# Input projections of a two-layer decoder as three float32r products, with low parts made by adding DMAs

## The chip, the core and the metric

The kernel runs on one core of a Trainium2 chip. The metric is the time of one execution on the device, in microseconds (us), and a version stands for the median of its runs.

## The reference

One sequence of 512 tokens with 1024 channels passes two layers. Layer 0 normalises x, projects it with one matrix of 1024 x 2560 and splits the columns into five blocks of 512: the input u of a state-space mixer, and query, forget, input (here: value) and gate of a gated linear recurrence. Layer 1 is sliding-window attention. Behind each mixer stands a mixture of 16 experts. What the change touches is the beginning:

```python
h = rms_norm(x, even_mix_norm[j])
proj = jnp.einsum('bld,de->ble', h, even_in_proj[j])
u = proj[..., :S5_WIDTH]
hq, hf, hi, hg = jnp.split(proj[..., S5_WIDTH:], 4, axis=-1)
a_out = s5_mixer(u, ...)            # step = exp(log_step); mag = exp(lam_re * step); scan over the sequence
b_out = hgrn2_mixer(hq, hf, hi, hg, ...)   # f = lb + (1 - lb) * sigmoid(hf); cumsum(log f) in chunks of 32
mix = jnp.einsum('blc,cd->bld', jnp.concatenate([a_out, b_out], axis=-1), even_out_proj[j])
```

All of it is float32, and the result must keep nearly that precision.

## The kernel before

Everything is written out by hand: each engine has one program, and the order of its instructions is the order in the text. Semaphores join them. SyncE issues the loads of a stream of weight slots (128 partitions x 2048 float32, 1 MB each) into a ring of six; a slot is loaded again when a counter (slot_free, w_lo_done) says that its last reader is done.

**Preparation.** x is loaded in four tiles of 128 tokens, normalised by ScalarE and VectorE, turned by TensorE and scaled by VectorE into hT (8 blocks of 128 channels x 512 tokens; `scaled`, line 1012). Meanwhile GpSimd works out the state-space coefficients on tiles of 128x16: step by `exact_exp` (line 439, a polynomial with some 25 small instructions), the turn (line 480), mag by the same function (line 481), mag to the fourth power (line 484), then turn_hi and turn_lo, and, once the constants are in, one product of 128x2048 (line 503, RAW).

**Products.** A block is 8 matmuls over the channel blocks, 128x512 out. Both operands are float32, which TensorE does in two passes, so that a product counts as two instructions. Four blocks make u (line 1763), and proj(i) makes blocks 0 to 3 of forget, 4 to 7 of query, 8 to 11 of value and 12 to 15 of gate (lines 1785 to 1805). ScalarE copies each result out of PSUM (lines 727 and 734).

**The order on TensorE** after u is: proj(0), turn_inputs (1770), proj(1), inputs(0) (1807), proj(2), proj(3), make_taps (1820), proj(4), inputs(1), proj(5), readout(0) (1832), proj(6), proj(7), readout(1), proj(8), readout(2), proj(9), readout(3), proj(10), proj(11). Then come the heads of the recurrence: head_scores(0) (1874), the first half of proj(12), head_increments(0) (1890), and so on, with the gate blocks between them, up to the gated linear unit (line 1929).

**VectorE** makes the coefficients (from line 1057; it waits there for mag), turned inputs and phases, then for four groups products_in, the scans and their products (scan_and_products, line 1189). scan 2 needs readout(0) done, scan 3 needs readout(1) done. `skip(b)` (line 1207) adds the readout to u. Behind skip(2) stands `forget` (1213), then, after ScalarE's Ln (line 779), the running sums (`summed_logs`, 1221). GpSimd's `differences(h)` (line 507) follow the sums, ScalarE's `exponentials(h)` (749) the differences, VectorE's `keyed(h)` (1245) the exponentials; head_scores(h) reads what they made. ScalarE's keys_out(0) stands behind exponentials(3), and head_increments(0) needs it.

**The three-product form** is in use elsewhere in the kernel (the output projection, line 1984, and the experts): an operand a is split into a_hi, its copy in float32r (a shorter mantissa, one pass on TensorE), made by ScalarE, and a_lo = a - a_hi, made by VectorE; hi x hi, hi x lo and lo x hi are summed in PSUM.

## Time and profile before

| | us |
|---|---|
| median of 3 runs | 839.35 (838.61 to 840.06) |
| the profiled execution | 841.01 |
| its span | 839.3 |
| TensorE, VectorE, ScalarE, GpSimd busy in the span | 788.5, 599.5, 467.2, 164.2 |
| mean granted clock of TensorE | 0.986 of 2.4 GHz |

The span is the time that the hardware profiler saw from the first to the last instruction, and the execution's own time is measured around it. Times in the rows below are microseconds from the start of the span. Busy time of TensorE is given twice, for matmuls (PE) and for the loads of their stationary operand (PEld). Instructions of one kind in a row are merged into one line with their count. Matmuls overlap at their ends, so a count of them is best divided out of the chain of waits, which has no overlap.

### The profile page before, as it was taken

How to read it: one execution, taken by the hardware profiler on the slowest of the kernel's cores; microseconds unless marked ns; L12 is line 12 of the kernel's file. 1: busy time of each engine (PE TensorE's matmuls, PEld its weight loads, DVE VectorE, ACT ScalarE, POOL GpSimd, SP SyncE). 2: the span in 40 equal slices, each digit the busy share in tenths (PEclk: the TensorE clock that was granted, in tenths of full speed). 3: DMA queues.
4: the chain of work that ended last, by engine and by line, in shares of the span. 5: the costliest groups of instructions: out<-in, count | busy, mean ns of one | idle time of the engine just before them, and what ended most of it. 6: DMA issues, size and time to landing. Idle time of an engine off the chain costs nothing.

```text
span 839.3 us, 11098 instructions
## 1 busy us (share of the span) xinstructions
PE 788.5 (94%) x4236; PEld 553.4 (66%) x4236; DVE 599.5 (71%) x817; ACT 467.2 (56%) x637; POOL 164.2 (20%) x169
## 2 busy tenths in 40 slices
PE   5999999999999899989999899999999899999993
PEld 3455555555588878867777455556579778777872
DVE  4699974866553779877987566667645688887891
ACT  5033202823432478776885219677735387787791
POOL 4400001500001223422211000133101223323221
PEclk9999999999999799999999999999999999999998
DMA  9421120203462499999995400052063599989962
GB/s 363 158 94 58 45 100 2 101 1 123 189 221 118 160 390 367 317 329 319 316 335 174 201 0 1 4 197 102 1 275 136 188 418 338 311 318 337 320 204 39
DMA packets 31450, 160.93 MB, mean 192 GB/s; under 512 B 7601, under 2 KB 7729, under 8 KB 16032
## 3 DMA queue, kind: packets, MB, share of 16 engines
q1 hardware_dynamic: 18432, 130.03, 40.6%
q0 software_dynamic: 11232, 24.60, 10.4%
q10 hardware_dynamic: 1728, 5.52, 1.8%
q8 instruction: 38, 0.62, 0.3%
q14 instruction: 20, 0.16, 0.1%
HBM read 152.32 MB, written 24.12 MB: 210 GB/s over the span
## 4 chain that ended last, share of the span: by engine, by line
PE 55%; DMA 18%; DVE 14%; ACT 8%; issue 1%; POOL 1%; DVEq 1%; ACTq 0%; POOLq 0%; SPq 0%
DMA ring<-stream 17%; PE PS L1797 11%; PE PS L1984 8%; DVE w_lo L994 8%; PE PS L2233 7%; PE PS L2114 5%; PE PS L1763 3%; ACT w_hi L688 3%; PE PS L2139 3%; PE PS L2014 2%; PE PS L2268 2%; PE PS L1929 2%; PE PS L2291 1%; PE PS L1747 1%; PE PS L2281 1%
## 5 line engine op out<-in xcount | busy, mean ns | idle before, releaser
L994 DVE TENSOR_TENSOR w_lo<-ring,w_hi 128x2048 fp32r<-128x2048 f32 x92 | 209.9, 2289 | 42.7 <-ACT w_hi L688 37.7
L688 ACT ACTIVATE w_hi<-ring 128x2048 fp32r<-128x2048 f32 x86 | 164.7, 1917 | 50.6 <-DMA ring<-stream 48.1
L2114 PE MATMUL PS<-w_hi,left_hi 128*128 128x512 f32 x512 | 174.6, 403 | 7.9 <-DVE w_lo L994 5.8
L2114 PEld LDWEIGHTS PS<-w_hi,left_hi 128*128 128x128 f32 x512 | 96.1, 188 | 31.5 <-DVE w_lo L994 5.8
L2114 PE MATMUL PS<-w_lo,left_hi 128*128 128x512 f32 x256 | 100.1, 391 | 0.0
L2139 PE MATMUL PS<-w_hi,left_lo 128*128 128x512 f32 x256 | 85.4, 394 | 9.1 <-DVE left_lo L994 7.9
L2233 PE MATMUL PS<-ring,hT 128*128 128x512 f32 (+1 forms) x192 | 73.5, 527 | 0.3 <-DVE hT L994 0.3
L536 POOL DMA_INDIRECT arena<-rows x32 | 47.6, 1488 | 121.6 <-PE PS L2091 106.1
L2139 PEld LDWEIGHTS PS<-w_hi,left_lo 128*128 128x128 f32 x256 | 48.0, 188 | 22.2 <-DVE left_lo L994 10.8
L1797 PE MATMUL PS<-ring,hT 128*128 128x512 f32 x128 | 57.6, 599 | 0.4 <-ACT arena L734 0.4
L1797 PE MATMUL PS<-hT,ring 128*128 128x512 f32 x128 | 56.3, 595 | 0.0
L2114 PEld LDWEIGHTS PS<-w_lo,left_hi 128*128 128x128 f32 x256 | 48.3, 189 | 8.3
L2233 PEld LDWEIGHTS PS<-ring,hT 128*128 128x128 f32 x192 | 34.7, 190 | 28.8 <-issue 26.9
L1984 PE MATMUL PS<-w_lo,left_hi 128*128 128x512 f32 x128 | 50.6, 396 | 0.3 <-DVE left_lo L994 0.3
L2139 PE MATMUL PS<-w_lo,left_lo 128*128 128x512 f32 x128 | 49.9, 390 | 0.0
L734 ACT ACTIVATE arena<-PS 128x512 f32<-128x512 f32 x16 | 9.6, 599 | 71.5 <-PE PS L1797 71.5
L1984 PE MATMUL PS<-w_hi,left_hi 128*128 128x512 f32 x112 | 44.8, 400 | 0.0
L994 DVE TENSOR_TENSOR left_hi<-PS,left_hi 128x1024 fp32r<-128x1024 f32 (+1 forms) x35 | 40.3, 1156 | 5.4 <-ACT left_hi L841 2.3
L1984 PE MATMUL PS<-w_hi,left_lo 128*128 128x512 f32 x112 | 43.8, 391 | 0.0
L1797 PEld LDWEIGHTS PS<-hT,ring 128*128 128x128 f32 x128 | 23.9, 190 | 28.9 <-issue 28.6
L1797 PEld LDWEIGHTS PS<-ring,hT 128*128 128x128 f32 x128 | 23.4, 190 | 27.3 <-issue 26.2
L540 POOL DMA_INDIRECT out<-hT,rows x16 | 26.0, 1627 | 68.7 <-ACT hT L857 68.7
(274 smaller groups left out, 1363.2 us busy)
## 6 DMA issues: line engine op xcount, KB each, us to landing
ring<-stream SPq DMA_DIRECT2D x110, 1024.0 KB, 16.3
arena<-stream SPq DMA_DIRECT2D x6, 1024.0 KB
rows<-arena POOLq DMA_DIRECT2D x8, 512.0 KB, 3.0
x<-stream SPq DMA_DIRECT2D x4, 1024.0 KB
x<-x_in SPq DMA_DIRECT2D x4, 512.0 KB, 5.8
x<-x_in ACTq DMA_DIRECT2D x4, 512.0 KB, 4.2
sums<-x POOLq DMA_DIRECT2D x4, 512.0 KB, 3.9
x<-sums SPq DMA_DIRECT2D x4, 512.0 KB, 5.4
```

Source lines behind the costliest of these rows:

```text
L536: return pool.indirect_dma_start(xrow[j], None, rows_d[:, :], bass.IndirectOffsetOnAxis(index, 0), bounds_check=SEQ - 1, oob_is_err=False)
L540: return pool.indirect_dma_start((sums_d, out_d)[layer][:, :], bass.IndirectOffsetOnAxis(index, 0), rows, None, bounds_check=SEQ - 1, oob_ ...
L688: act.activation(w_hi[pair], held_slot(layer, m), ACT.Copy).then_inc(w_hi_done, 1)
L994: return V.tensor_tensor(out, a, b, op)
L1763: ins = mm(PS[:, 2 + cb % 2, :], k512(k // 4)[:, k % 4, cb * 128:cb * 128 + 128], hT[:, k, :], start=k == 0, stop=k == KD - 1)
L1797: ins = mm(PS[:, 7 if i >= 12 else 6 + i % 2, :], lhsT[:, m], rhs, start=k == 0, stop=k == KD - 1)
L1929: ins = mm(PS[:, (0, 1, 4, 5)[b], :], k512(GLU0)[:, k, b * 128:b * 128 + 128], catT[:, k, :], start=k == 0, stop=k == 3)
L1984: ins = mm(mixed(layer, s // 2, tt), a, b, start=k == 0 and n == 0, stop=k == KD - 1 and n == 2)
L2014: ins = mm(PS[:, 2 + tt % 2, 0:20], tokT[tt % 2][:, k, :], w[:, k, :], start=k == 0, stop=k == KD - 1)
L2114: ins = mm(PS[:, gate_bank(e), :], a, b, start=k == 0 and t == 0, stop=k == KD - 1 and t == 2)
L2139: ins = mm(PS[:, y_at(layer, e) + half, :], a, b, start=k == 0 and t == 0, stop=k == 1 and t == 2)
L2233: ins = mm(PS[:, 2 + part, 0:n], hT[:, k, tt * 128:tt * 128 + 128], w, start=k == 0, stop=k == KD - 1)
```

## The change

u is still made of four blocks, but only the first stays a float32 product. The other three, and the blocks of forget, query and value, become three float32r products each: w_hi x h_hi, w_hi x h_lo, w_lo x h_hi. Blocks are numbered j = 0 to 3 for u, 4 to 11 for forget and query; the stream's slots of these three are laid out block by block (half a slot, 128x1024, is one block), and forget comes first in the stream while u is loaded first.

**High parts** are copies by ScalarE: `block_hi(j)`. hT_hi takes the place of x, its two halves are copied by ScalarE and VectorE. **h_lo** is written by VectorE over hT itself, which is possible once block 0 is done.

**Low parts of the weights** are made without VectorE: ScalarE writes -w_hi (`block_minus`), and a DMA issued by GpSimd adds the weights to it from DRAM (accumulate), 512 KB a block. GpSimd issues `block_lo(j)` when in_split says that -w_hi is there and when the one before it has landed. The value weights go the same way with all their 2 MB in one DMA (V_LO). The gate blocks 12 to 15 stay float32 and need hT again: one more adding DMA of 2 MB, from SBUF to SBUF, makes h_lo + h_hi (HT_BACK) when block 11 is done, and both GpSimd's differences(0) (which overwrites hT_hi) and proj(12) wait for it.

**mag** moves from GpSimd to VectorE, between its copy of hT and its first use. In the router the semaphores gaps_done, flags_done and weighed become one counter, weigh_done.

```diff
 (SyncE)
-            for j in range(RING):
+            for j in (2, 3, 0, 1, 4, 5):
                 sp.dma_start(slot(j), stream_d[j, :, :]).then_inc(slot_full[j], 16)
 (GpSimd)
-            exact_exp(mag, t2, t0, t1, mag_step)
-            nc.gpsimd.tensor_tensor(mag_step, mag, mag, ALU.mult)
+            def block_lo(j):
+                pool.wait_ge(in_split, 2 * j)
+                if j >= 2:
+                    pool.wait_ge(in_lo_in, 16 * (j - 1))
+                at = 1024 * (j % 2)
+                pool.dma_start(ring_split[:, in_place(j)], stream_d[(2, 0, 4)[j // 4] + j % 4 // 2, :, at:at + 1024], accum_op=ALU.add)\
+                    .then_inc(in_lo_in, 16)
...
+            block_lo(1)
             pool.wait_ge(const_rest, 48)
             pool.wait_ge(turned_psum, 2 * TT)
...
                                     turn_hi.unsqueeze(2).to_broadcast([P, PAIRS, NSTEP]), ALU.mult).then_inc(turns_done, 1)
+            for j in range(2, 12):
+                block_lo(j)
+            pool.wait_ge(in_split, 26)
+            pool.wait_ge(in_lo_in, 16 * 11)
+            pool.dma_start(ring_split[:, 0:2 * SLOT].rearrange("p (s n) -> p s n", n=SLOT), stream_d[6:8, :, :].rearrange("s p n -> p s n"),
+                           accum_op=ALU.add).then_inc(in_lo_in, 16)
+            pool.wait_ge(proj_psum, 12)
+            pool.wait_ge(in_lo_in, 16 * V_LO)
+            pool.dma_start(left_flat_lo.bitcast(f32), hi_flat.bitcast(f32), accum_op=ALU.add, max_dma_last_dim=4096).then_inc(in_lo_in, 16)
...
             pool.wait_ge(state_done, 4)
+            pool.wait_ge(in_lo_in, 16 * HT_BACK)
             differences(0)
 (ScalarE)
+            block_hi(1)
+            act.wait_ge(hT_done, 2 * TT)
+            act.activation(hT_hi[:, 0:4, :], hT[:, 0:4, :], ACT.Copy).then_inc(hT_split, 1)
...
+            block_minus(1)
+            for j in (2, 3):
+                block_hi(j)
+                block_minus(j)
...
+            block_hi(4)
+            block_minus(4)
             for cb in range(4):
...
+            for j in range(5, 9):
+                block_hi(j)
+                block_minus(j)
...
             projected(0)
+            projected(1)
+            block_hi(9)
+            block_minus(9)
...
-            for i in range(1, 10):
+            for i in range(2, 10):
                 projected(i)
+                if i in (2, 3):
+                    block_hi(8 + i)
+                    block_minus(8 + i)
+                if i == 7:
+                    for s in range(2):
...
+                        act.activation(v_hi(s), slot(6 + s), ACT.Copy).then_inc(in_split, 1)
+                    act.drain()
+                    for s in range(2):
+                        act.activation(v_lo(s), v_hi(s), ACT.Copy, scale=-1.0).then_inc(in_split, 1)
 (VectorE)
+            V.tensor_copy(hT_hi[:, 4:8, :], hT[:, 4:8, :]).then_inc(hT_split, 1)
...
+            ts(e_p, e_r, 1.0 / 5040, ALU.mult)
+            for c in (1.0 / 720, 1.0 / 120, 1.0 / 24, 1.0 / 6, 0.5, 1.0):
+                dve.drain()
+                stt(e_p, e_p, c, e_r, ALU.add, ALU.mult)
...
+            dve.wait_ge(u_psum, 1)
+            for half in range(2):
+                ks = slice(4 * half, 4 * half + 4)
+                dve.wait_ge(hT_split, 2)
+                tt_(left_lo[:, ks, :], hT[:, ks, :], hT_hi[:, ks, :], ALU.subtract).then_inc(hT_split, 1)
 (TensorE)
+            def block_products(j, out, terms=(0, 1, 2)):
+                for t in terms:
+                    if t == 0:
+                        pe.wait_ge(in_split, 2 * j - 1)
+                    if t == 2:
+                        pe.wait_ge(in_lo_in, 16 * j)
+                    w, h = (in_hi(j), in_hi(j), in_lo(j))[t], (hT_hi, left_lo, hT_hi)[t]
...
+            for cb in range(1, 4):
+                block_products(cb, PS[:, 2 + cb, :], (0,))
+            for cb in range(1, 4):
+                block_products(cb, PS[:, 2 + cb, :], (1, 2)).then_inc(u_psum, 1)
...
-            proj(0)
+            split_proj(0)
+            split_proj(1)
             turn_inputs()
-            proj(1)
+            split_proj(2)
...
             inputs(0)
-            proj(2)
-            proj(3)
+            split_proj(3)
+            pending[0] = 2
+            split_proj(4)
             make_taps()
-            proj(4)
+            split_proj(5)
             inputs(1)
-            proj(5)
+            split_proj(6)
+            split_proj(7)
+            pending[0] = 2
             readout(0)
-            proj(6)
-            proj(7)
+            split_values(8, (0, 1))
+            split_values(9, (0, 1))
+            split_values(8, (2,))
+            split_values(9, (2,))
             readout(1)
-            proj(8)
+            split_values(10, (0, 1, 2))
+            split_values(11, (0, 1, 2))
+            pending[0] = 4
             readout(2)
-            proj(9)
             readout(3)
-            proj(10)
-            proj(11)
```

pending is the number of slots that the next block's first matmul gives back to SyncE.

## Rows read from the trace of the kernel before

**Rows 1.** The page, busy time of each engine.
```profile
PE 788.5 (94%) x4236; PEld 553.4 (66%) x4236; DVE 599.5 (71%) x817; ACT 467.2 (56%) x637; POOL 164.2 (20%) x169
```

**Rows 2.** Windows: length, busy time (instructions) of PE, PEld, DVE, ACT, POOL, clock, DMA share, GB/s.
```profile
16.40:161.00 144.60, 144.57 (x916) 75.94 (x916) 114.37 (x174) 42.77 (x61) 26.45 (x46) 1.00 0.24 88
...
44.20:65.00 20.80, 20.80 (x192) 12.81 (x190) 20.20 (x12) 9.94 (x13) 0.00 (x0) 1.00 0.18 64
...
91.00:118.00 27.00, 27.00 (x156) 13.68 (x149) 24.37 (x47) 4.01 (x5) 0.00 (x0) 1.00 0.12 40
```

**Rows 3.** The chain of waits over the span, merged: start, length, engine and line.
```profile
16.43 27.70 PE PS L1763 x64
...
235.08 27.27 PE PS L1984 x120
```

**Rows 4.** The chain of waits from 140 to 166 us.
```profile
140.96 1.92 ACT arena L779
...
142.91 1.24 DVE arena L1224
...
144.28 1.84 POOL x L511
...
160.73 0.49 ACT arena L761
```

**Rows 5.** Timeline of TensorE: start, length, line, operation.
```profile
130.01 1.94 PE L1846 MATMUL PS<-arena 128*32 128x127 f32 x64
...
161.91 1.17 PE L1899 MATMUL PS<-arena 32*128 32x128 f32 x30
```

**Rows 6.** Timeline of GpSimd and VectorE, 17 to 35 us.
```profile
17.73 0.28 POOL L442 TENSOR_SCALAR small<-small 128x16 f32<-128x16 f32 x1
...
27.38 0.22 POOL L484 TENSOR_TENSOR small<-small 128x16 f32<-128x16 f32 x1
...
28.07 0.17 DVE L997 TENSOR_SCALAR small<-small 128x16 f32<-128x16 f32 x1
...
28.32 0.44 DVE L994 TENSOR_TENSOR small<-small,param 128x16 f32<-128x16 f32 x4
...
31.09 3.81 POOL L503 TENSOR_TENSOR xs<-const,small 128x2048 f32<-128x2048 f32 x1 [0.21 <-issue]
```

**Rows 7.** Timeline: 128x2048 operations on VectorE and ScalarE.
```profile
49.40 1.22 DVE L997 TENSOR_SCALAR xs<-xs 128x2048 f32<-128x2048 f32 x1
...
53.07 2.29 DVE L994 TENSOR_TENSOR xs<-const,small 128x2048 f32<-128x2048 f32 x1
...
90.02 1.91 ACT L777 ACTIVATE arena<-arena 128x2048 f32<-128x2048 f32 x1
```

**Rows 8.** Windows of 2 us, columns as in rows 2: the first loads.
```profile
18.00:20.00 2.00, 2.00 (x6) 0.82 (x5) 0.32 (x2) 1.81 (x4) 1.22 (x6) 1.00 1.00 415
...
28.00:30.00 2.00, 2.00 (x6) 0.95 (x5) 1.63 (x10) 0.00 (x0) 1.29 (x5) 1.00 0.36 138
```

**Rows 9.** The page, DMA queues and issues.
```profile
q1 hardware_dynamic: 18432, 130.03, 40.6%
q0 software_dynamic: 11232, 24.60, 10.4%
...
rows<-arena POOLq DMA_DIRECT2D x8, 512.0 KB, 3.0
```

**Rows 10.** Windows at the end: the last adding store alone.
```profile
831.00:835.00 4.00, 0.00 (x0) 0.00 (x0) 0.00 (x0) 0.00 (x0) 0.00 (x0) 0.63 0.51 74
832.00:834.00 2.00, 0.00 (x0) 0.00 (x0) 0.00 (x0) 0.00 (x0) 0.00 (x0) 0.52 0.54 96
```

**Rows 11.** Windows: the lower clock.
```profile
276.00:278.00 2.00, 2.00 (x11) 2.00 (x11) 1.67 (x6) 0.88 (x1) 0.85 (x2) 0.50 0.58 227
...
284.00:286.00 2.00, 2.00 (x25) 1.94 (x24) 1.79 (x6) 0.00 (x0) 0.00 (x0) 0.51 0.00 0
```

**Rows 12.** Timeline of GpSimd: the longest issue of a gather.
```profile
340.94 3.08 POOL L536 DMA_INDIRECT arena<-rows x1 [4.65 <-PE PS L2091]
```

171 lines of the change are left out of this document (126 added, 45 removed).

## The prediction

> **What bounds the kernel now.** I read the page first: TensorE is busy 94% of the span, VectorE 71%, ScalarE 56%, GpSimd 20% [rows 1]. The change lies in the first layer's input stage, so the windows of that stage come next: from 16.4 to 161 us TensorE has no gap, and VectorE is nearly as full from 44 to 118 us [rows 2]. The chain of waits, merged over the whole span, agrees: its longest piece here is the 27.70 us of the 64 float32 passes of line 1763 (32 products of 128x512) [rows 3]. A product costs 27.70 / 32 = 0.866 us, a block of 8 costs 6.93 us.
>
> The chain in detail shows the part that a reader misses in the shares [rows 4]. Around 143 us it leaves TensorE: Ln on ScalarE, the first running sum on VectorE, then GpSimd's differences from 144.28 us, ScalarE's exponentials, and at 160.73 the copy of the keys, which releases head_increments(0) on TensorE at 161.91. From the start of differences(0) to that product are 17.63 us, and TensorE has no say in them. TensorE's float32 products happened to fill that time. So TensorE's saving reaches the end only as far as **differences(0) starts before 144.28**.
>
> **The change, part by part.**
>
> Products. Three float32r products of a k step cost 3 x 27.27/120 = 0.682 us against 0.866 [rows 3]; 24 + 96 steps change, so TensorE loses 120 x 0.184 = 22 us of work. But the chain passes through the end of readout(2), at 131.95 now (130.01 + 1.94) [rows 5]. Before it stand 13 blocks of 6.93 = 90.1 us; afterwards 1 x 6.93 + 15 x 5.45 = 88.7, three blocks more having been moved ahead of it. **131.95 becomes 130.6 if nothing waits.**
>
> mag on VectorE. It takes GpSimd's second exponential away (17.73 to 27.6 us [rows 6]) and puts some 18 dependent steps on VectorE, each about 0.26 us with its drain as in 28.07 to 28.32 [rows 6]: 4.8 us. They start near 20, after VectorE's half of the copy of hT (128x2048, an estimated 1.5 us, between the 1.22 us of a scalar operation and the 2.29 of a two-operand one [rows 7]), and end near 25, before GpSimd's 27.6. Then come two differences for left_lo, 2 x 2.29, ending near 31.1. VectorE's coefficients move by about 1.7 us; their cover is TensorE's own blocks, which reach turn_inputs only near 56 us, and without this cover they would cost these 1.7 us.
>
> ScalarE gets 11 pairs of 128x1024 copies (1.0 us each, half of the 1.91 of a 128x2048 one [rows 7]) and four of 128x2048, 30 us in all. It is free for most of the stage; only the last four are on the path (below).
>
> The semaphores of the second group (weigh_done) cost nothing: the waits are the same ones on the same engine's order. The order of the loads likewise: the queues are drained at about 29 us in any order [rows 8], and slot 2 is the first now.
>
> Accumulating DMAs. This is the disputed price. A plain 512 KB store from GpSimd lands 3.0 us after issue [rows 9]; its data take 1.26 us at the 415 GB/s of the first loads [rows 8], so 1.74 is fixed. No row shows an accumulation into SBUF. The nearest are the expert stores, which add into DRAM. Lower bound, plain speed: 2 MB in 5.05 + 1.74 = 6.8 us, 512 KB in 3.0. Upper bound, the last store alone on the queues: from 831 to 835 us a share of 0.51 moves 74 GB/s, that is 74/0.51 = 145 GB/s at full share (96/0.54 = 178 in its middle) [rows 10]: 14.6 + 1.74 = 16.3 us and 5.4. A third reading is queue 0 over the span: 24.60 MB in 10.4% of 839.3 = 87.3 us of 16 engines [rows 9]. 8.4 MB are plain stores (16 of 512 KB), the rest divides by 32 gathers to 30 adding stores, 8.4 and 7.8. Taking the plain 16.8 MB at queue 1's 381 GB/s (130.03 MB in 40.6%) leaves 43 us for 7.8 MB: 181 GB/s. I take **181, since it averages 30 stores: 13.3 us for 2 MB, 4.7 for 512 KB**.
>
> The Trainium skill, "Collectives: The Full Stack", section "The bandwidth ceiling: the fold count and why AG ≠ RS ≠ AR", says that a reduce isn't slowed by the add but by its two reads, which halve the rate. The trace shows more than half lost; by that rule 2 MB would take 10.1 + 1.74 = 11.8 us and the result below would be about 3 us lower.
>
> Now the waits, walked along each engine:
> - Block 1's low part is issued at 22.2 and lands in time. Left_lo costs TensorE 1.3 us. Then GpSimd itself waits: the constants land near 30.5 (queues drained at 29 [rows 8]), its 3.81 us multiplication [rows 6] stands ahead of the second accumulation, which is issued at 34.4 and lands at 39.1. TensorE is there at 35.7: 3.4 us idle. The third, queued behind the second's landing, lands at 43.9: 1.1 idle. From there 4.7 us a block is less than TensorE's 5.45. One wait of 1.5 us for projected(0), now behind eight copies on ScalarE, follows near 61. Together 7.3: readout(2) would end at 137.9.
> - Value weights. Block 11 ends at 104.1. Only then does ScalarE write v_hi and v_lo (0.6 + 4 x 1.95), and the 2 MB accumulation can be issued at 112.4: it lands at 125.7. Behind readout(0) TensorE has four products' worth of cover (4 x 1.82), until 115.4. **10.3 us idle**. Readout(1), and with it VectorE's last scans, stand behind it: readout(2) ends at 148.2.
> - HT_BACK. Issued when the twelfth block is done, 4.0 us before that: 144.2. At that moment the change also gives back four slots at once, 4.2 MB of loads (10 us at 415), and they share the queues: I add half, 5 us (bounds 0 and 10). It lands near 162.6, and differences(0) waits for it. Without it Ln, forget and the sum would allow 148.2 + 0.75 + 3.2 + 1.9 + 1.4 = 155.5.
>
> **Sum:** differences(0) from 144.28 to 162.7, +18.4, and 0.2 for the exponentials behind it: +18.6. The profiled run took 841.01 (span 839.3), 1.7 over the median 839.35; I add to the median: 858. The clock stood at its lower level (0.50 of 2.4 GHz) for some 10 us after the small router products and it is low in the mean of the last store's window, behind the last product [rows 10, 11]; two pauses of over 10 us may bring it in. I count nothing for it and leave up to 5 us in the range.
>
> **Rivals.**
> 1. Accumulations near plain speed (6.8 and 3.0 us). Then idle falls to 1.8 at the second block and 3.8 at the values, HT_BACK hides behind Ln, and differences(0) starts at 146.4: +2.4, 841.8. For it: the destination is SBUF, and the direct form fills all 16 engines. Against: both readings of the adding stores. Chance 0.20, a quarter of it within 0.2%.
> 2. They are heavier (16.3 and 5.5) and the four loads go first (10): +31, 870. GpSimd issues them while VectorE is full, and a gather's issue took 3.08 us where the usual is 1.0 [rows 12]. The Trainium skill, "DMA: Bandwidth & Descriptors", section "SWDGE vs HWDGE vs iDMA", has a reason: VectorE's two-port modes lock GpSimd out of the memory in which the descriptors are written; no row here shows that this is the cause. Chance 0.11.
> 3. Faster: every accumulation is hidden. The place is the values' low part, where the 10.3 us vanish if it lands 3 us after its issue; with all transfers free the walk gives differences(0) at 141.6, **-2.4, 837**. That is the most the chain through forget, Ln and the exponentials lets out of 22 us. It decides from about 4.5 us for 2 MB, less than the plain 5.05 of data. Chance 0.09, of which 0.02 ends within 0.2%.
>
> **How the numbers follow.** Forecast case 0.60. 0.2% is 1.7 us, about what a measurement of this kernel can tell. Slower: 0.60 + 0.15 + 0.11 = 0.86; same 0.05 + 0.02 = 0.07; faster 0.07. The range starts at 841 with most of rival 1 in it and ends at 871, rival 2.
>
> **What would show it.** TensorE idle in front of the third product (low part) of block 2 (3 to 4 us near 36), and about 10 us in front of split_values' third term near 115, released by queue 0; GpSimd's first difference at 155 or later, released by a DMA; 120 x 3 products at 0.227 us. The windows should have TensorE idle about 17 us before the heads and again while the exponentials run. I am wrong if 2 MB land within 7 us of their issue, or if differences(0) is released by VectorE.

## The result, and the profile after

The changed kernel takes **871.48 us** (868.89 to 873.81, 4 runs) where the kernel before took 839.48 on the same chip: ratio 1.038 (95% interval 1.034 to 1.042). It is slower by 32.0 us. The profiled execution took 873.5 us, its span is 871.7.

The page of the changed kernel, busy time of each engine, queue 0 (packets, MB, share), and DMA issues (KB of one, median us from issue to landing):

```profile
PE 778.6 (89%) x4356; PEld 581.3 (67%) x4356; DVE 607.6 (70%) x838; ACT 500.6 (57%) x664; POOL 160.5 (18%) x156
...
q0 software_dynamic: 13616, 34.56, 16.3%
...
ring_split<-stream POOLq DMA_DIRECT2D x11, 512.0 KB, 5.5
...
ring_split<-stream POOLq DMA_DIRECT2D x1, 2048.0 KB, 13.4
left_lo<-hT_hi POOLq DMA_DIRECT2D x1, 2048.0 KB, 24.6
```

TensorE is busy 10 us less than before [rows 1], although the span is 32 longer: it stands still. The waits of TensorE from 16 us up to the output projection, in total us, times and the longest, say where:

```profile
PE PS L2051 <- DVE x L1091: 21.9, 1, 21.9
PE PS L1946 <- DMA ring_split<-stream: 10.2, 1, 10.2
PE PS L1897 <- DMA ring_split<-stream: 7.6, 5, 4.1
PE PS L1961 <- ACT arena L817: 3.3, 1, 3.3
PE PS L1897 <- ACT arena L817: 1.6, 1, 1.6
PE PS L1897 <- DVE left_lo L1091: 0.8, 1, 0.8
```

L1897 are the blocks, L1946 the value blocks, L2051 head_scores(0), L1961 proj(12). And the chain of waits from 100 to 190 us, which answers to [rows 4]:

```profile
99.69 11.12 PE PS L1897 x48
...
115.11 3.73 ACT ring_split L871 x2
...
119.12 13.36 DMA ring_split<-stream
...
132.53 6.50 PE PS L1946 x16
139.03 2.16 PE PS L2004 x8
141.18 1.87 PE PS L2012 x64
143.05 11.16 PE PS L1946 x48
...
154.50 24.61 DMA left_lo<-hT_hi
...
179.24 1.06 POOL x L565
```

Read it downwards: ScalarE's -v_hi, the 2 MB adding DMA V_LO, 16 products at a mean granted clock of 0.57 (the lower level, 1.2 GHz, is 0.50), readout(1), the last value blocks, then the second 2 MB adding DMA HT_BACK, and only then GpSimd's differences(0) at 179.24 instead of 144.28, 34.96 us later. Nearly all of it, 34.4 us, stands at the long piece of the output projection (269.46 against 235.08 [rows 3]); some two are given back behind it, where the chain of both kernels runs through the loads of the experts' weights (ring<-stream).

### The profile page after: what moved, and what is told of

It reads as the page before. It is cut to its first block, busy times and chain, and to the rows that moved or that the text cites. A ratio compares the mean times of both kernels' runs of the same rounds, so it can differ in the third digit from the quotient of the medians.

```text
span 871.7 us, 11403 instructions
## 1 busy us (share of the span) xinstructions
PE 778.6 (89%) x4356; PEld 581.3 (67%) x4356; DVE 607.6 (70%) x838; ACT 500.6 (57%) x664; POOL 160.5 (18%) x156
## 4 chain that ended last, share of the span: by engine, by line
PE 52%; DMA 23%; DVE 8%; ACT 7%; issue 4%; POOL 2%; POOLq 2%; ACTq 1%; DVEq 0%; SPq 0%
DMA ring<-stream 16%; PE PS L2155 8%; PE PS L2404 7%; PE PS L2285 7%; PE PS L2310 5%; PE PS L1897 4%; DVE w_lo L1091 4%; PE PS L1961 4%; DMA ring_split<-stream 3%; DMA left_lo<-hT_hi 3%; ACT w_hi L743 3%; PE PS L1946 2%; PE PS L2185 2%; PE PS L2439 2%; PE PS L2100 2%
## 5 line engine op out<-in xcount | busy, mean ns | idle before, releaser
L2310 PE MATMUL PS<-w_hi,left_lo 128*128 128x512 f32 x256 | 87.5, 403 | 7.2 <-DVE left_lo L1091 6.0
L591 POOL DMA_INDIRECT arena<-rows x32 | 39.5, 1233 | 129.0 <-PE PS L2262 115.6
L2404 PEld LDWEIGHTS PS<-ring,hT 128*128 128x128 f32 x192 | 35.3, 193 | 29.6 <-issue 27.7
L1897 PE MATMUL PS<-hT_hi,ring_split 128*128 128x512 f32 x144 | 39.0, 420 | 9.1 <-DMA ring_split<-stream 7.6
L2155 PE MATMUL PS<-w_hi,left_lo 128*128 128x512 f32 x112 | 43.8, 391 | 0.0
L1897 PEld LDWEIGHTS PS<-hT_hi,ring_split 128*128 128x128 f32 x144 | 28.1, 201 | 17.6 <-DMA ring_split<-stream 9.7
L1097 DVE SCALAR_TENSOR_TENSOR arena<-const,PS 128x256 f32<-128x256 f32 x64 | 26.4, 475 | 17.5 <-PE PS L2439 17.5
L681 POOL TENSOR_TENSOR arena<-arena,small 128x1024 f32<-128x1024 f32 x8 | 15.2, 1896 | 121.7 <-DVE small L1779 121.7
## 6 DMA issues: line engine op xcount, KB each, us to landing
ring_split<-stream POOLq DMA_DIRECT2D x1, 2048.0 KB, 13.4
left_lo<-hT_hi POOLq DMA_DIRECT2D x1, 2048.0 KB, 24.6
```

The lines of the kernel that those rows point to most:

```text
L591: return pool.indirect_dma_start(xrow[j], None, rows_d[:, :], bass.IndirectOffsetOnAxis(index, 0), bounds_check=SEQ - 1, oob_is_err=False)
L1097: return V.scalar_tensor_tensor(out, a, s, b, op0, op1)
L1897: ins = mm(out, w[:, k, :], h[:, k, :], start=t == 0 and k == 0, stop=t == 2 and k == KD - 1)
L2155: ins = mm(mixed(layer, s // 2, tt), a, b, start=k == 0 and n == 0, stop=k == KD - 1 and n == 2)
L2310: ins = mm(PS[:, y_at(layer, e) + half, :], a, b, start=k == 0 and t == 0, stop=k == 1 and t == 2)
L2404: ins = mm(PS[:, 2 + part, 0:n], hT[:, k, tt * 128:tt * 128 + 128], w, start=k == 0, stop=k == KD - 1)
```

## The experiments

The runs are numbered in the order in which they were made, as the expectations call them. Each is compared with the kernel before on the same chip (its median was 838.7 to 839.8). "differences(0)" is the start of GpSimd's first difference in the profiled execution. Such a start is one execution's: readout(0) began at 110.63 us in the profile of the changed kernel and at 108.91 to 109.80 in those of runs 1, 2, 3, 4, 9 and 11, whose TensorE program is the same up to there. A difference of one or two microseconds between two profiles shows nothing by itself.

**What HT_BACK costs (runs 1 and 3).** Two edits, one at a time. Run 1 gives the four slots back later, so that no loads run beside HT_BACK:

```diff
             split_values(11, (0, 1, 2))
-            pending[0] = 4
             readout(2)
...
             head_scores(0)
+            pending[0] = 4
             proj(12, low)
```

> The changed kernel, with the four slots given back at proj(12)'s first matmul instead of readout(2)'s, so that no load runs beside HT_BACK. Theory A (the four loads share the queues and stretch HT_BACK from about 13.4 us, the value weights' time, to 24.6): HT_BACK lands 13 to 15 us after its issue, differences(0) starts at about 169 instead of 179.2, the time falls by 9 to 11 us to about 861. Theory B (an addition from SBUF to SBUF is slow by itself): HT_BACK still takes over 20 us and the time falls by less than 4 us.

861.91 us, 1.027 (1.023 to 1.032). GpSimd's timeline of this run:

```profile
151.38 1.31 POOL L558 DMA_DIRECT2D left_lo<-hT_hi  x1 [32.78 <-PE PS L1946]
166.08 1.06 POOL L565 TENSOR_TENSOR x<-arena 128x512 f32<-128x512 f32 x1 [13.39 <-DMA left_lo<-hT_hi]
```

The landing takes 14.6 us instead of 24.6, and the time is 9.6 us less: of 32 us, the collision of one transfer with four loads costs 10. (Differences(0) comes 13.2 us earlier; 3.1 of these were there at the issue of HT_BACK, which the edit doesn't touch.) Windows of both kernels, first the changed one, then run 1 (length, busy time of PE, PEld, DVE, ACT, POOL, clock, DMA share, GB/s):

```profile
163.00:176.00 13.00, 0.00 (x0) 0.00 (x0) 5.23 (x5) 2.40 (x2) 0.00 (x0) 0.59 1.04 309
```

```profile
155.00:163.00 8.00, 4.34 (x77) 3.11 (x72) 5.77 (x8) 3.19 (x2) 0.00 (x0) 1.00 1.05 181
```

The queues are full in both. Alone, the adding DMA moves 181 GB/s; with plain loads beside it the sum is 309. The two queues of the changed kernel from 160 to 176 us (packets, MB, share of 16 engines):

```profile
q0 software_dynamic: 424, 1.74, 54.2%
q1 hardware_dynamic: 433, 3.15, 49.5%
```

The adding DMA (q0) and the loads (q1) halve the engines' time between them, and the adding DMA is the one that ends last.

Run 3 takes HT_BACK out and lets VectorE add:

```diff
-            pool.dma_start(left_flat_lo.bitcast(f32), hi_flat.bitcast(f32), accum_op=ALU.add, max_dma_last_dim=4096).then_inc(in_lo_in, 16)
...
             scan_and_products(3)
+            for half in range(2):
+                at = slice(2048 * half, 2048 * half + 2048)
+                dve.wait_ge(proj_psum, 12)
+                tt_(hT_t[:, at], left_flat_lo[:, at], hi_flat[:, at], ALU.add).then_inc(hT_split, 1)
             skip(2)
```

> The changed kernel, with hT restored by VectorE (two additions of 128x2048, 4.6 us, ahead of skip(2)) instead of HT_BACK. Theory A (differences(0) waits for HT_BACK and for nothing else that late): it starts when Ln and the first sum allow, near 166.5, 12.7 us earlier; TensorE's pause before the heads is shorter by as much; time 857 to 859. Rival (the loads of 4 MB or the exponentials set the heads anyway): less than 5 us.

860.23, 1.025 (1.020 to 1.031), a little over the expected 857 to 859; differences(0) at 164.33, released by VectorE's first sum. It comes 14.9 us earlier and head_increments(0) 12.1 (184.87 against 196.97): the time follows the second.

**What V_LO costs (runs 2 and 4).** In run 2 V_LO is replaced by two subtractions of 128x2048 on VectorE, behind scan 2:

```diff
-            pool.dma_start(ring_split[:, 0:2 * SLOT].rearrange("p (s n) -> p s n", n=SLOT), stream_d[6:8, :, :].rearrange("s p n -> p s n"),
-                           accum_op=ALU.add).then_inc(in_lo_in, 16)
...
             scan_and_products(2)
+            for s in range(2):
+                dve.wait_ge(in_split, 23 + s)
+                tt_(v_lo(s), slot(6 + s), v_hi(s), ALU.subtract).then_inc(hT_split, 1)
```

> The changed kernel, with the low parts of the value weights made by VectorE (2 subtractions of 128x2048 behind scan 2, 2.29 us each) instead of two copies by ScalarE and the 2 MB adding DMA. Theory A (the wait of 10.2 us before split_values' third product and the low clock behind it, 6.50 us for 16 products that take 3.63 at full clock, are on the path): readout(2) ends 12 to 13 us earlier, near 145.5, and the time falls to about 859. Rival (HT_BACK alone decides, since it is issued by a count of blocks): it moves with the twelfth block and so by the same amount; if only the wait of 10.2 counts and not the clock, the fall is 10 us, to 861.5; if the values' DMA hid something else, under 5 us.

867.83, 1.034 (1.029 to 1.038): a miss. The median is 3.7 us under the changed kernel's and the ranges overlap; differences(0) is at 174.03, 5.2 us earlier. TensorE's wait in this run:

```profile
126.93 6.88 PE L1942 MATMUL PS<-ring_split,hT_hi 128*128 128x512 f32 x16 [6.16 <-DVE ring_split L1084]
```

A wait for VectorE stands in the place of the one for the DMA. Run 4 has the edits of runs 2 and 3 together:

> Both: value weights' low parts and hT by VectorE, the eleven 512 KB adding DMAs stay. If the two costs add up (Theory A): 871.5 - 12.5 - 13.5 = 845 to 847, differences(0) near 153.5, still some 9 us after the 144.3 of the kernel before, because the chain of block DMAs holds readout(0) until 114.8 and readout(2) until about 145. If they overlap: 855 or more.

857.62, 1.022 (1.018 to 1.027), differences(0) at 160.16. My expectation missed by 11 us, and the time is that of its rival. VectorE's timeline of this run, the order of what follows readout(0) and, from 148 us, what stands ahead of forget:

```profile
113.38 0.75 DVE L1087 SCALAR_TENSOR_TENSOR arena<-arena,param,PS 128x512 f32<-128x512 f32 x1 [4.54 <-PE PS L2009]
114.22 2.49 DVE L1081 TENSOR_TENSOR arena<-PS,xs 128x512 f32<-128x512 f32 x4
...
124.66 4.49 DVE L1081 TENSOR_TENSOR ring_split<-ring,ring_split 128x2048 fp32r<-128x2048 f32 x2
137.38 0.75 DVE L1087 SCALAR_TENSOR_TENSOR arena<-arena,param,PS 128x512 f32<-128x512 f32 x1 [8.24 <-PE PS L2009]
...
148.50 4.49 DVE L1081 TENSOR_TENSOR hT<-left_lo,hT_hi 128x2048 f32<-128x2048 f32 x2 [3.89 <-PE PS L1943]
```

VectorE is idle for 4.54 us, then does other work while v_hi (ready from 113) waits; TensorE waits for the subtractions, and scan 3 (138) waits for TensorE's readout(1). The last series tests this.

**The price of the accumulation (run 8).** All thirteen adding DMAs as plain copies, everything else the same; the kernel leaves out the subtraction of w_hi and the addition of h_hi:

```diff
-                pool.dma_start(ring_split[:, in_place(j)], stream_d[(2, 0, 4)[j // 4] + j % 4 // 2, :, at:at + 1024], accum_op=ALU.add)\
+                pool.dma_start(ring_split[:, in_place(j)], stream_d[(2, 0, 4)[j // 4] + j % 4 // 2, :, at:at + 1024])\
...
-            pool.dma_start(left_flat_lo.bitcast(f32), hi_flat.bitcast(f32), accum_op=ALU.add, max_dma_last_dim=4096).then_inc(in_lo_in, 16)
+            pool.dma_start(left_flat_lo.bitcast(f32), hi_flat.bitcast(f32), max_dma_last_dim=4096).then_inc(in_lo_in, 16)
```

> The changed kernel with the accumulation left out of all its thirteen DMAs of the input stage (same source, destination, size and waits, but a plain copy), which prices the add itself. The computation leaves out: the subtraction of the high part, so that the low parts are the weights themselves, and h_hi in what is given back to hT. By the theory that the accumulation costs the rate (181 GB/s and less), 512 KB land in 3.0 to 3.3 us and 2 MB in 6.8 (from 5.5 and 13.4): V_LO's idle time falls from 10.2 us to about 3.6, block 11 ends 4 to 6 us earlier, HT_BACK beside 4 MB of loads lands in 10 to 15 us, and the time is 848 to 853. By the rival that GpSimd's issue and the fixed part set the times (the descriptors, with VectorE full), 512 KB stay above 4.5 us and 2 MB above 11, and the time is 865 or more.

854.65, 1.019 (1.017 to 1.021), 1.7 us over the expected range, with every transfer a little slower than expected. Its DMA issues:

```profile
ring_split<-stream POOLq DMA_DIRECT2D x11, 512.0 KB, 3.9
...
ring_split<-stream POOLq DMA_DIRECT2D x1, 2048.0 KB, 7.8
left_lo<-hT_hi POOLq DMA_DIRECT2D x1, 2048.0 KB, 17.8
```

The add costs 1.6 us of 5.5 and 5.6 of 13.4. But without it the kernel is still 16 us slower than before, so the adding rate is only half of the story. Windows of V_LO with the queues full, here the changed kernel and then the plain copy:

```profile
122.00:130.00 8.00, 0.34 (x2) 0.00 (x0) 4.09 (x7) 0.00 (x0) 0.00 (x0) 0.65 1.01 209
```

```profile
117.00:120.00 3.00, 0.73 (x4) 0.26 (x2) 2.92 (x7) 0.00 (x0) 0.00 (x0) 0.96 1.03 407
```

V_LO adds from DRAM at 209 GB/s, HT_BACK (run 1) from SBUF at 181, a copy moves 407. V_LO's packets are of 8 KB and HT_BACK's of 4 KB, so that the source is not the only difference, and no run parts the two.

**The lower clock (run 9).** 40 matmuls that nobody reads, in TensorE's pause for V_LO, on top of run 3:

```diff
+            for n in range(40):
+                mm(PS[:, 5, :], hT_hi[:, 0, 0:128], v_hi(0)[:, 0:512], start=True, stop=True)
             split_values(8, (2,))
```

> The kernel of the third run (hT given back by VectorE, V_LO still an adding DMA) with 40 matmuls whose result nobody reads in front of the value blocks' third term, where TensorE is idle for about 10 us. They are 40 x 0.227 = 9.1 us long, so they end before V_LO lands; the work left to do is the same. The 16 products behind the wait took 6.5 us in the changed kernel where 16 elsewhere take 3.63. By the theory that this is TensorE's lower clock after the pause they take 3.6 to 3.8 now and readout(2), hence differences(0), comes 2.5 to 3 us earlier (164.3 to about 161.6): 857 to 858, where the third run had 860.2. By the rival that the products are slow because their operands come out of the DMA's last bytes or VectorE is full, they stay near 6.3 and the time at 860.

TensorE's timeline without them (run 3), and with them:

```profile
131.01 6.45 PE L1947 MATMUL PS<-ring_split,hT_hi 128*128 128x512 f32 x16 [10.08 <-DMA ring_split<-stream]
```

```profile
121.34 9.23 PE L2038 MATMUL PS<-ring_split,hT_hi 128*128 128x512 f32 x40
131.51 3.94 PE L1947 MATMUL PS<-ring_split,hT_hi 128*128 128x512 f32 x16 [0.94 <-DMA ring_split<-stream]
```

2.5 us less for the same 16 products, differences(0) at 162.32 instead of 164.33 (though readout(0) had begun 0.6 later). 859.05 us, 1.024 (1.021 to 1.027): the median is 1.2 us under run 3's, and their ranges overlap, so the shift is shown by the trace and not by the time. The granted clock over the 16 products is 1.00, where run 3 has 0.57.

**Low parts by GpSimd (runs 5 to 7).** Run 5 is run 4 with the last adding DMAs gone: GpSimd itself subtracts, 128x1024 a block (those of blocks 2 and 3 ahead of its multiplication), and ScalarE writes no -w_hi.

```diff
-                pool.dma_start(ring_split[:, in_place(j)], stream_d[(2, 0, 4)[j // 4] + j % 4 // 2, :, at:at + 1024], accum_op=ALU.add)\
-                    .then_inc(in_lo_in, 16)
+                nc.gpsimd.tensor_tensor(in_lo(j), in_raw(j), in_hi(j), ALU.subtract).then_inc(in_lo_in, 16)
...
-                act.drain()
-                act.activation(in_lo(j), in_hi(j), ACT.Copy, scale=-1.0).then_inc(in_split, 1)
```

> The kernel of the fourth run (value low parts and hT by VectorE) whose eleven 512 KB adding DMAs are taken out too: GpSimd writes each low part in place as the slot minus its high part (128x1024), and ScalarE writes no negative copies. No adding DMA is left in the input stage; nothing of the computation is left out. By the theory that block 11 ended 6.5 us late (110.6 against the 104.1 of the walk) because each adding DMA took 5.5 us where 4.7 were counted, a subtraction of 128x1024 on GpSimd, an estimated 1.9 us by half of the 3.81 of its 128x2048 product, keeps TensorE free of waits for blocks 2 to 11: block 11 ends near 103, seven us or so earlier than in the fourth run, and differences(0) starts 4 to 6 us earlier, at 154 to 156: 852 to 854. The rival: the idle time of blocks 2 to 11 is TensorE's clock or ScalarE's copies and stays; then 857 to 858 as in the fourth run.

871.94, 1.039 (1.037 to 1.041): 14 us slower than the run it was built on, the largest miss. The timelines of GpSimd and then VectorE in this run, from 21 us:

```profile
21.56 4.76 POOL L523 TENSOR_TENSOR ring_split<-ring,in_hi 128x1024 fp32r<-128x1024 f32 x2 [0.21 <-issue]
```

```profile
21.78 2.28 DVE L1081 TENSOR_SCALAR small<-small 128x16 f32<-128x16 f32 x2
24.14 2.22 DVE L1160 CAST small<-small 128x16 int32<-128x16 f32 x1
26.43 2.27 DVE L1078 TENSOR_TENSOR small<-small 128x16 f32<-128x16 f32 x1
...
37.00 4.49 DVE L1078 TENSOR_TENSOR left_lo<-hT,hT_hi 128x2048 fp32r<-128x2048 f32 x2 [0.17 <-issue]
```

A step of 128x16 on VectorE takes 2.2 us, nearly the 2.38 of one GpSimd subtraction, where it takes 0.25 alone: VectorE stands until GpSimd's instruction is over. left_lo begins at 37.0 instead of 24.82, and TensorE is idle for 11.05 us (and for another 6.2 later, in front of make_taps, which waits for VectorE). The Trainium skill, "SBUF — State Buffer", section "Who interferes with whom", says that a VectorE operation with two SBUF inputs and a GpSimd operation that reads SBUF exclude each other, and that the first holds the pair for its whole instruction. The rows agree for VectorE's subtraction at 26.43, which has two such inputs; the TENSOR_SCALAR and the CAST in front of it were held just as long.

The next two runs kept GpSimd's subtractions. Run 6, forget ahead of the additions and of skip(2):

```diff
             scan_and_products(3)
+            forget()
...
                 tt_(hT_t[:, at], left_flat_lo[:, at], hi_flat[:, at], ALU.add).then_inc(hT_split, 1)
-            skip(2)
-            forget()
             summed_logs(0)
             summed_logs(1)
+            skip(2)
```

> The kernel of the run before this one, with VectorE's order changed behind scan 3: forget, then the two additions that give hT back, then the first two running sums, then skip(2) (before: additions, skip(2), forget, sums). TensorE's order stays. The theory that the time is set by when differences(0) starts expects it 3 to 6 us earlier (the additions of 4.5 us lie beside ScalarE's Ln, and skip(2)'s wait for readout(2) is behind): 847 to 850. The rival, that TensorE is the bound again as soon as the adding DMAs are gone, expects no change from the run before it, within 1 us.

863.01, 1.028 (1.025 to 1.031): 8.9 us from VectorE's order alone, more than the 3 to 6 expected, though the time itself is 13 us over the expected one, as run 5's loss stays in it. Run 7, the value low parts on GpSimd as well:

```diff
-                tt_(v_lo(s), slot(6 + s), v_hi(s), ALU.subtract).then_inc(hT_split, 1)
...
+                nc.gpsimd.tensor_tensor(v_lo(s), slot(6 + s), v_hi(s), ALU.subtract).then_inc(in_lo_in, 16)
```

> The kernel of the run before this one, with the value blocks' low parts (two subtractions of 128x2048) on GpSimd, which has nothing to do from block 11 on, instead of on VectorE behind scan 2. In the second run they came late on VectorE (from 124.7 us, where TensorE stood at 122.3), and that is my reason for its small gain. By this theory the first lands about 4 us behind v_hi, near 117, the second near 121, TensorE is not idle in front of the value blocks' third term (6.2 us in the second run), readout(2) ends 5 to 7 us earlier, and with it differences(0): 841 to 845. The rival, that these idle microseconds are covered again by VectorE's own scans 2 and 3 (which VectorE has still to do before forget), expects at most 2 us of gain.

858.07, 1.022 (1.020 to 1.024). TensorE has no wait in front of the values' third term (16 products in 3.88 us), but block 11 ends near 123 us as in run 6 (109.1 in run 4). The time is 13 us over the expected 841 to 845, since run 5's loss is still in it. The step itself gave 4.9 us (differences(0) at 163.42 against 167.93): near the theory's 5 to 7, over the rival's 2.

**Single parts (runs 16, 15 and 10).** Run 16, block 2's adding DMA in front of GpSimd's wait for the constants:

```diff
             block_lo(1)
+            block_lo(2)
             pool.wait_ge(const_rest, 48)
...
-            for j in range(2, 12):
+            for j in range(3, 12):
```

> The changed kernel with one edit: block 2's adding DMA stands in front of GpSimd's wait for the constants and its multiplication of 128x2048, instead of behind them. By the prediction's step it was late by that wait: it is issued near 28 when block 1's has landed (36.5 in the changed kernel), lands near 34, and TensorE's 4.1 us of idle time in front of block 2's low part goes, along with most of the lower clock's 1.5 us; block 3's DMA is issued near 34 to 37. As every later DMA waits for the one before it, the whole row moves forward by up to 5 us: block 11 ends at 105 to 107 (110.6), and differences(0) at 174 to 176 (179.2): 867 to 869. The rival, that the DMAs' own pace of 5.8 us a block holds the blocks anyway and VectorE's work behind readout(0) has no need of them, expects 870 to 872.

868.84, 1.035 (1.031 to 1.038), differences(0) at 174.48, both as expected. The ranges of this run and the changed kernel overlap; readout(0) begins at 106.68, 2.2 us before the earliest of the other runs. GpSimd's timeline of this run:

```profile
22.11 1.10 POOL L526 DMA_DIRECT2D ring_split<-stream  x1 [0.72 <-ACT ring_split L788]
32.73 0.87 POOL L526 DMA_DIRECT2D ring_split<-stream  x1 [9.52 <-DMA ring_split<-stream]
```

The second DMA cannot be issued before 32.7, since the first lands only then: ten microseconds for 512 KB, in the crowd of the first loads.

Run 15, mag alone, as an edit of the kernel before:

```diff
-            exact_exp(mag, t2, t0, t1, mag_step)
...
+            tt_(mag, e_p, e_k, ALU.mult)
```

> The kernel before with one edit: mag and its fourth power are made by VectorE (18 dependent steps at 128x16) and no more by GpSimd. My prediction gave this 4.8 us on VectorE, ending near 25 where GpSimd ended at 27.6, and cost it at nothing because TensorE reaches the work that needs it much later. Expected: VectorE's first use of mag at 23 to 25 in place of 27.70, GpSimd's multiplication of 128x2048 a few us earlier, and the same time, 838 to 840. The rival, that the input stage is bound by VectorE from 44 us on and so starts and ends earlier, expects 835 to 837.

839.79, 1.001 (0.999 to 1.003): no difference. GpSimd's multiplication began only 1.2 us earlier, at 29.89, as it waits for the constants.

Run 10, forget and two sums ahead of skip(2) in the kernel before:

```diff
             scan_and_products(3)
-            skip(2)
             forget()
             summed_logs(0)
             summed_logs(1)
+            skip(2)
```

> The kernel before, with one edit: VectorE does forget and the first two running sums ahead of skip(2), whose wait for readout(2) holds them back. Nothing is left out. My account says that TensorE is the bound up to head_increments(0) and that the chain from differences(0) lies beside its float32 products; the trace also has ScalarE's Ln behind the copy of proj(9) in the program's order, at 140.96, so that forget has 5 us to spare anyway. By that the time stays: 839 to 840, differences(0) at 143 to 144.3. The rival, that the chain from forget to the exponentials bounds the kernel before too, expects 835 to 837.

838.56, 1.000 (0.998 to 1.001); differences(0) at 143.83, only 0.45 earlier. So the kernel before is not bound by this order.

**Where TensorE's saving ends (runs 11 to 14, 17 and 18).** The last series starts from run 4 (blocks' low parts by adding DMAs, values and hT by VectorE) and changes the order alone, each run on top of the one before it. Run 11 has run 6's order behind scan 3, and the value subtractions earlier:

```diff
+            for s in range(2):
+                dve.wait_ge(in_split, 23 + s)
+                tt_(v_lo(s), slot(6 + s), v_hi(s), ALU.subtract).then_inc(hT_split, 1)
             products_in(3)
             scan_and_products(2)
```

> The kernel of the fourth run (blocks' low parts by adding DMAs, value low parts and hT by VectorE) with VectorE's order mended in two places: the two value subtractions ahead of products_in(3) instead of behind scan 2, and forget ahead of the additions, skip(2) behind the first two sums. No work is added or left out. By the theory that the fourth run lost its gain to the order (TensorE idle 6.2 us for subtractions at 124.7, then at the lower clock, 16 products in 6.3 us; skip(2) and the additions in front of forget), TensorE has no wait at the values, readout(2) ends near 144, the additions 144, differences(0) starts near 145 to 147 (160.2 in the fourth run): 842 to 846. The rival, that VectorE's added 9 us simply move its scans and forget back, expects differences(0) at 151 or later: 849 to 852.

Run 12, TensorE's readouts (and the value subtractions behind products_in(3), the first sum ahead of the additions):

```diff
             split_proj(6)
+            readout(0)
             split_proj(7)
             pending[0] = 2
-            readout(0)
+            readout(1)
...
             split_values(9, (2,))
-            readout(1)
```

> The kernel of the run before this one, with readout(0) in front of forget-and-query's last block and readout(1) behind it (they were behind that block and behind the value blocks 8 and 9), the value subtractions behind products_in(3), the first running sum in front of the additions, the additions' second half first, and GpSimd's differences(0) waiting for that half alone (ScalarE's exponentials wait for the other). No work is added or left out. VectorE's 4.5 us of waiting for readout(0) and its wait for readout(1) go. Expected by the theory that all is decided by the start of differences(0): 141 to 143 against 144.28 in the kernel before, and 836 to 840. By the rival that some 3 us more of idle TensorE and low clock behind it are paid at the heads, or that the stage is bound by block 11 at 109 and VectorE's own work: 841 to 845.

Run 13, the gate block ahead of the heads, and ScalarE's copies likewise:

```diff
+            proj(12, low)
             head_scores(0)
-            proj(12, low)
             head_increments(0)
```

> The kernel of the twelfth run (readouts first) with the first half of proj(12) in front of head_scores(0) instead of behind it, ScalarE's copies of blocks 10 and 11 in front of the exponentials, and its keys_out(0) in front of exponentials(3). No work is added or left out. In the twelfth run TensorE is idle for 6.8 us in front of head_scores(0) and then does these 8 matmuls in 4.7 us (3.7 at full clock) ahead of head_increments(0) at 163.4. By the theory that the end follows head_increments(0) and that only this order delays it, they lie in the idle time, head_increments(0) comes at 159.5 to 160.5, and the time is 835.5 to 837 (twelfth run 839.4, the kernel before 838.9). By the rival that ScalarE's and VectorE's own chain (exponentials, keyed) ends at 162 or later, or that the loss comes back in the heads, 838.5 to 839.5.

Run 14, the whole of it:

```diff
             proj(12, low)
+            proj(12, high)
             head_scores(0)
             head_increments(0)
-            proj(12, high)
```

> As the run before this one, but with both halves of proj(12) in front of head_scores(0). The time in front of head_scores(0) is long enough for both (from about 148.6 to 155.4), and TensorE has 3.6 us less to do behind head_increments(0). If TensorE alone bounds the heads, another 2 to 3.5 us are gained: 832.5 to 835. If head_scores(1) and the states of the first head then have to be waited for (the rival), the gain of the run before this one stays as it is, within 1 us.

Run 17, ScalarE:

```diff
             exponentials(3)
+            projected(12)
+            keys_out(1)
             for b in range(4):
...
-            for h in range(HEADS - 1):
+            output_out(0)
+            for h in range(1, HEADS - 1):
```

> The fourteenth run's kernel with ScalarE's copies of proj(12) and of the second head's keys in front of the four Gelu operations instead of behind them. No work is added or left out. By the theory that the gain stopped at this order, proj(13) starts near 163 to 164 (167.1 in the fourteenth run, 168.4 in the kernel before), the gated linear unit starts 3 to 5 us earlier than the 204.5 of the kernel before, and the time is 834 to 836. If the glu starts that early and the time stays above 838, the rest of the kernel (weights' loads behind it) takes the gain back; if the glu stays at 204 or later, another wait has taken the place of this one: also 838 to 841.

Run 18 adds the edit of run 16:

> The run before this one with block 2's adding DMA in front of GpSimd's wait for the constants and its multiplication, as in the sixteenth run, which started differences(0) 4.8 us earlier in the changed kernel and gained 2.6 us of time. Here VectorE has less slack behind the blocks, so I expect differences(0) 2 to 4 us earlier than in the run before it and 1 to 3 us of time: 831.5 to 835. The rival, that ScalarE's and VectorE's work sets the heads now, expects no difference within 1 us.

Starts in the profiled executions, in us, and the times (the "glu" is the gated linear unit, the first piece behind the heads):

| run | differences(0) | head_increments(0) | glu | median | ratio (interval) |
|---|---|---|---|---|---|
| before | 144.28 | 161.91 | 204.56 | 838.7 to 839.8 | 1 |
| 4 | 160.16 | 180.32 | 222.32 | 857.62 | 1.022 (1.018 to 1.027) |
| 11 | 146.13 | 163.35 | 205.35 | 839.63 | 1.001 (0.998 to 1.004) |
| 12 | 143.57 | 163.37 | 205.37 | 839.39 | 1.000 (0.998 to 1.003) |
| 13 | 142.87 | 158.34 | 204.19 | 839.87 | 1.001 (0.999 to 1.002) |
| 14 | 142.71 | 157.39 | 205.31 | 841.47 | 1.003 (1.002 to 1.005) |
| 17 | 142.73 | 157.42 | 199.85 | 834.57 | **0.995** (0.993 to 0.997) |
| 18 | 140.23 | 154.91 | 197.44 | 833.09 | **0.992** (0.989 to 0.995) |

Order alone takes 18 us off (run 11, 2 us better than expected), and TensorE has no wait at the values. Then the gain stops. Runs 13 and 14 missed: head_increments(0) came at 158.34 and 157.39, earlier than expected, but the glu stayed where it was and the time too, in run 14 even a little over the kernel before. So beyond run 12 an earlier differences(0) or head_increments(0) no longer sets the time. Two places show why. In run 12, TensorE's timeline has it idle for the heads, with the gate block behind:

```profile
155.43 2.07 PE L2050 MATMUL PS<-x 128*128 128x128 f32 x8 [6.79 <-DVE x L1083]
158.78 4.66 PE L1960 MATMUL PS<-ring,hT 128*128 128x512 f32 x8 [0.43 <-ACT arena L810]
```

In run 13 these products fill the pause, the other half of proj(12) then runs at the lower clock (5.60 us in place of 3.70), and ScalarE's order is next: the copy of proj(12), which frees the PSUM bank of proj(13), stands behind the Gelus and two loads of a table:

```profile
160.88 1.28 ACT L878 ACT_TABLE_LOAD   x1
162.17 3.91 ACT L878 ACTIVATE arena<-arena 128x512 f32<-128x512 f32 x4
166.10 1.28 ACT L810 ACT_TABLE_LOAD   x1
167.40 0.60 ACT L810 ACTIVATE arena<-PS 128x512 f32<-128x512 f32 x1
```

In run 14 it shows as TensorE's wait, and in run 17 the same matmuls start 3.5 us earlier:

```profile
167.06 5.82 PE L1960 MATMUL PS<-ring,hT 128*128 128x512 f32 x8 [3.66 <-ACT arena L810]
```

```profile
163.51 3.89 PE L1963 MATMUL PS<-ring,hT 128*128 128x512 f32 x8
```

Runs 17 and 18 met their expectations: they beat the kernel before by 4.5 and 5.9 us. (Run 17's and run 18's intervals overlap; the step between them stands in the trace, 2.4 us at the glu.)

## Why the prediction was off

Its direction and, for this kernel, its mechanism held: the start of differences(0) decides the time, the two 2 MB adding DMAs are on the path, and TensorE's saved work is no gain. (Where differences(0) came before 144.28, in runs 12 to 14, it no longer did; the prediction's "TensorE's saving reaches the end only as far as differences(0) starts before 144.28" names a condition that was not enough.) The time came out just above the range (871.48 against 871), 13.4 us above the forecast. By its own steps:

| step | forecast | measured |
|---|---|---|
| block 11 ends | 104.1 | 110.6 |
| V_LO issued | 112.4 | 119.12 |
| V_LO, issue to landing | 13.3 | 13.4 |
| TensorE idle for it | 10.3 | 10.2 |
| the 16 products behind it | 3.63 | 6.50 |
| HT_BACK issued | 144.2 | 154.50 |
| HT_BACK, issue to landing | 18.3 | 24.6 |
| differences(0) | 162.7 | 179.24 |
| from there to head_increments(0) | 17.6 | 17.7 |

Three terms of the sum were mis-sized, and a fourth was right by luck.

**Block 11, 6.5 us.** The trace has 10.0 us of waits where I had 7.3, and 3.8 us of low clock where I had none (three groups of 8 products: 3.60, 3.33 and 2.40 less 3 x 1.83). "Block 1's low part is issued at 22.2 and lands in time" failed:

```profile
32.44 3.60 PE L1897 MATMUL PS<-hT_hi,ring_split 128*128 128x512 f32 x8 [1.87 <-DMA ring_split<-stream]
41.97 3.33 PE L1897 MATMUL PS<-hT_hi,ring_split 128*128 128x512 f32 x8 [4.11 <-DMA ring_split<-stream]
```

It was issued at 22.03 into queues which were full until 31 us here (rows 8 showed them full until about 29), and landed near 32.4. I had counted those full queues for the constants and not for this DMA. It also shared them with the constants: GpSimd had these at 32.65 (30.5 forecast; 29.89 in run 15, without this DMA), and so issued block 2's low part at 36.52 and not at 34.4. "From there 4.7 us a block is less than TensorE's 5.45" failed as well, at a small price: the low parts land in 5.5 and are mostly issued every 5.7 to 6.0, as each waits for the one before it, and the waits behind block 2's come to 1.6 us where I had 1.1. Of the 6.5 us, 0.8 to 1.7 are this one execution's, by the other runs' readout(0).

**The lower clock, 2.9 us on the path behind V_LO,** and with the blocks' 3.8 nearly 7. I counted nothing and left 5 in the range. The granted clock was 0.57 over these products, and run 9, with the pause filled, shows it to be the pause's doing. The size varies: the same 16 products took 5.35 us in run 1 and 5.72 in run 16.

**HT_BACK, 6.3 us.** "I add half, 5 us (bounds 0 and 10)": the loads cost the full 10, by run 1 (14.6 against 24.6), as the adding DMA got half of the engines' time and ended last. The other 1.3 us are its own 14.6 where I had 13.3.

**V_LO, 13.4 us against 13.3, is luck.** The rate was taken too low (181 against 209 GB/s), which is 1.6 us too much, and the fixed part too small: 13.4 less the 10.0 us of its data leave 3.4 us, and 5.5 less 2.5 leave 3.0 for 512 KB, where I had 1.74. That came from the fastest of the plain 512 KB stores (rows<-arena, 3.0 us); two others in the same trace took 3.9 (below) and 4.0 (out<-x):

```profile
sums<-x POOLq DMA_DIRECT2D x4, 512.0 KB, 3.9
```

The three sum to 6.5 + 2.9 + 6.3 = 15.7 of the 16.5 us by which differences(0) is late; the rest lies in the issue of HT_BACK. Some 3 us of the 16.5 did not reach the time, which is 13.4 over the forecast.

Of the rivals, the second had the time (870) with half of its reason. The loads cost the 10 us that it gave them, though they did not go first but shared the engines; the adding rate from DRAM was 209 GB/s, not 145. The first needed plain speed; even with plain copies the time was 854.65 and not its 842, since it left out the collision (HT_BACK landed in 17.8 us beside the loads), block 1 and the clock as well. The third, a gain of 2.4 us by hidden transfers, took more than hiding: without either of the 2 MB DMAs (run 4) it was 857.6, and only the new order of four engines brought 833 to 835. No run had all transfers free in the order as it stood, so that my ceiling of 837 for it is untested; runs 17 and 18 went under it with another order.

The small steps held: mag on VectorE ended at 22.1 (25 forecast) and cost nothing, alone as in the whole; left_lo cost 0.8 us (1.3 forecast). The Trainium skill's rule on a reduce ("Collectives: The Full Stack", "The bandwidth ceiling: the fold count and why AG ≠ RS ≠ AR"), two reads and half the rate, was nearer than my own reading: 209 against 407 GB/s is 0.51 for V_LO, and 181 is 0.44 for HT_BACK.

## What to carry over

An adding DMA is a transfer with a rate of its own, here 0.44 to 0.51 of a copy's, and what is put on the queues beside it makes it longer, here by the whole time of four loads: give buffers back after it has landed, not when it is issued. A fixed part is read from more than one row. When work taken off the busiest engine brings nothing, follow the chain of waits to the instruction that stands in front of the late one on its own engine. Two of the adding DMAs had to go, and the orders of VectorE, TensorE (twice), ScalarE and GpSimd had to change, before an estimated 22 us less of TensorE's work became 5.9 us less of time.

## What the runs showed of the hardware

- With the queues full, an adding DMA moved 209 GB/s from DRAM into SBUF (8 KB packets) and 181 from SBUF into SBUF (4 KB packets); a plain copy 407. From issue to landing, 3.0 to 3.4 us came on top of the data's own time (2.6 for the plain copies).
- Beside four plain loads of 1 MB, an adding DMA of 2 MB got half of the 16 engines' time and landed in 24.6 us instead of 14.6.
- GpSimd's subtractions and its multiplication hold VectorE up until they end, small steps too: 128x16 in 2.2 us instead of 0.25. The trace of before had one such place: VectorE's four products of 128x512 at 29.5 us took 5.94 us beside GpSimd's multiplication, 2.49 in the changed kernel. There the multiplication meets twelve 128x16 steps instead, which take 5.13 us (1.71 in run 15).
- TensorE's next 16 products took 5.35 to 6.50 us behind pauses of 10 us for V_LO, 6.88 and 6.29 behind pauses of 6.2 (runs 2 and 4, where VectorE had made the operand), and 3.94 with the pause filled. Behind short pauses the runs differ: 8 products took 3.46 us behind one of 0.71 (run 4) and 2.12 behind one of 1.07 (run 11).
